# Attention's small products moved between input-projection tiles, the samples' RWKV step made a thread of the merged stage, and a written-out order table

## What is computed

```python
h = rms_norm(x, norm_mix_pre); proj = h @ w_in
q, kv_rows, win_rows, gates = nsa_project(proj[..., :NSA_PROJ], pos)      # rope on q and k, gates = sigmoid
kc, vc = compress(kv_rows[..., 0]), compress(kv_rows[..., 1])             # blocks of 32 rows, stride 16: w1, gelu, w2
o_nsa = g0 * attend(q, kc, vc) + g1 * attend_selected_blocks + g2 * attend_window
o_rwkv = rwkv_time_mix(proj[..., NSA_PROJ:])    # s = s*w + (s a) b + v k;  y = s r;  norm, gate
x = x + rms_norm(concat(o_nsa, o_rwkv) @ w_out)
x = x + rms_norm(conv_ffn(rms_norm(x)))         # conv of width 3, gelu, times value
```

## Time and profile before

| what | us |
|---|---|
| median of 3 runs | 2395.59 (2394.9 to 2395.8) |
| the profiled execution's own time | 2394.03 |
| span of its trace | 2392.2 |
| PE busy, share of the span | 2031.3, 85% |
| DVE busy | 1236.8, 52% |
| ACT busy | 715.2, 30% |
| mean granted TensorE clock | 0.919 of 2.4 GHz |

### The profile page before, as it was taken

How to read it: one execution, slowest core, us unless ns; L and a number is a source line. 1 busy time by engine, 2 the same in 40 slices (tenths; PEclk the granted TensorE clock), 3 DMA queues, 4 the chain that set the end, 5 groups by cost and what they waited for, 6 DMA issues and landing times.

```text
span 2392.2 us, 54387 instructions
## 1 busy us (share of the span) xinstructions
PE 2031.3 (85%) x22574; PEld 1861.8 (78%) x22574; DVE 1236.8 (52%) x1984; ACT 715.2 (30%) x1320; POOL 159.9 (7%) x233
## 2 busy tenths in 40 slices
PE   4997598988877899999669966989787769999995
PEld 3996587855666899999669956877566659999994
DVE  4222667778654544452332237687776454444422
ACT  3221123333333332332132221333342332222421
POOL 1000111111100001000010001110101000010000
PEclk9997699979988999999879977999899979999997
DMA  3346133223322232223122552322333212232231
GB/s 110 97 105 208 40 104 90 72 70 107 100 68 65 71 93 93 90 88 98 48 80 93 126 170 61 102 72 72 89 102 102 68 47 89 89 97 90 89 98 66
DMA packets 172769, 216.43 MB, mean 90 GB/s; under 512 B 39009, under 2 KB 138594, under 8 KB 171106
## 3 DMA queue, kind: packets, MB, share of 16 engines
q1 hardware_dynamic: 172514, 212.87, 29.7%
HBM read 204.57 MB, written 16.59 MB: 92 GB/s over the span
## 4 chain that ended last, share of the span: by engine, by line
PE 61%; DVE 18%; SPq 11%; issue 5%; ACT 3%; DMA 1%; DVEq 0%; ACTq 0%
PE ps L833 16%; PE ps L835 16%; PE ps L834 16%; SPq L713 9%; PE ps L1156 2%; PE ps L901 1%; SPq L709 1%; PE ps L874 1%; DVE x L2101 1%; PE ps L1129 1%; DVE arena L1916 1%; DVE arena L1925 1%; PE ps L1037 1%; DVE hf_lo L1654 1%; DVE arena L1690 1%
## 5 line engine op out<-in xcount | busy, mean ns | idle before, releaser
L833 PE MATMUL ps<-hm_hi,ring_hi 128*128 128x260 f32 x2432 | 694.5, 286 | 44.2 <-DVE hm_lo L1654 44.2
L835 PE MATMUL ps<-hm_hi,ring_lo 128*128 128x260 f32 x2432 | 692.3, 285 | 0.0
L834 PE MATMUL ps<-hm_lo,ring_hi 128*128 128x260 f32 x2432 | 690.3, 284 | 0.0
L1647 DVE TENSOR_TENSOR ring_lo<-ring,ring_hi 128x1024 fp32r<-128x1024 f32 x200 | 244.9, 1226 | 698.4 <-ACT ring_hi L1308 697.7
L833 PEld LDWEIGHTS ps<-hm_hi,ring_hi 128*128 128x128 f32 x2432 | 463.7, 191 | 47.9 <-issue 47.9
L834 PEld LDWEIGHTS ps<-hm_lo,ring_hi 128*128 128x128 f32 x2432 | 463.2, 190 | 0.0
L835 PEld LDWEIGHTS ps<-hm_hi,ring_lo 128*128 128x128 f32 x2432 | 463.1, 190 | 0.0
L1308 ACT ACTIVATE ring_hi<-ring 128x1024 fp32r<-128x1024 f32 x200 | 211.9, 1060 | 687.1 <-PE ps L835 674.6
L833 PE MATMUL ps<-hf_hi,ring_hi 128*128 128x260 f32 x704 | 202.2, 287 | 8.8 <-DVE hf_lo L1654 8.2
L835 PE MATMUL ps<-hf_hi,ring_lo 128*128 128x260 f32 x704 | 200.6, 285 | 0.0
L834 PE MATMUL ps<-hf_lo,ring_hi 128*128 128x260 f32 x704 | 200.5, 285 | 0.0
(11 more groups left out here) (377 smaller groups left out, 3235.3 us busy)
## 6 DMA issues: line engine op xcount, KB each, us to landing
ring<-in_w SPq DMA_DIRECT2D x202, 512.0 KB, 3.6
arena<-in_kv_cmp SPq DMA_DIRECT2D x96, 128.0 KB, 2.3
extra<-in_kv_cmp SPq DMA_DIRECT2D x80, 128.0 KB, 2.3
slot<-in_kv_cmp SPq DMA_DIRECT2D x80, 128.0 KB, 2.1
out_win_old<-in_win SPq DMA_DIRECT2D x16, 511.0 KB, 9.3
slot<-in_k_sel SPq DMA_DIRECT2D x96, 64.0 KB, 1.9
arena<-in_k_sel SPq DMA_DIRECT2D x96, 64.0 KB, 1.9
extra<-in_v_sel SPq DMA_DIRECT2D x96, 64.0 KB, 1.9
```

The costliest lines, as they stand in the source:

```text
L833: mmul(out, wh, hi[:, k, cols], start=(k == 0), stop=False)
L834: mmul(out, wh, lo[:, k, cols], start=False, stop=False)
L835: last = mmul(out, wl, hi[:, k, cols], start=False, stop=(ci == len(chunks) - 1 and k == k1 - 1))
L1647: v.tensor_tensor(ring_lo[:, n % RING, :], r, ring_hi[:, n % RING_HI, :], SUB).then_inc(S["w_lo"], 1)
```

## The change

- The 24 gate columns become a 25th full tile of the input projection, behind the attention tiles. ACT takes its tanh on the way out; PE transposes it.
- Gate transposes, rope, value transposes and the prompt's compression are given to PE, ACT and DVE between the RWKV tiles, one item behind each tile (`beside`). Their PSUM banks are 6 and 7. The compression takes the samples' paired form: 16 products instead of 64, its gelu written out with tanh and DVE operations.
- SP loads compression weights, rope table and the samples' state behind the chunk 3, and waits for the page table later. Two sample units are loaded ahead instead of three. Old window rows are copied between the sample units, after every second one.
- The samples' RWKV step becomes 23 steps in the merged order (`one_step`, `step_thread`); RWKV's first super-chunk waits for it; its two stores are issued by ACT.
- The order is written out as 750 digits, one thread number per step; the search at build time is gone.
- POOL no longer clears compression weights.

```diff
-C_IN, C_GATE = 0, NT + RP
-C_OUT = C_GATE + 1
+C_IN, N_IN = 0, NT + 1 + RP
+C_OUT = N_IN
...
-        put("mix", "DVE", 0.7, ago("rkv"))
+        put("mix", "DVE", 0.7, *([ago("rkv")] if sc else []))
+        if sc == 0:
+            key, engine, us, _ = front.pop()
+            front.append((key, engine, us, [("rs", 0, "out")]))
...
         put = into(back)
         put("scaled", "DVE", 2.72, ago(("solve", 1)), *here("exps", "keys"))
+        if sc == 0:
+            back[-1][3].append(("rs", 0, "store"))
...
+def step_thread():
+
+    out = []
+    for name, engine, us, *after in (
+            ("mix", "DVE", 2.4), ("tanh", "ACT", 0.8, "mix"), ("small", "PE", 2.6, "tanh"), ("sig", "ACT", 2.2, "small"),
+            ("root", "ACT", 0.4, "small"), ("prep", "DVE", 2.8, "sig", "root"), ("pin", "ACT", 0.4, "sig"), ("rk", "PE", 0.3, "prep"),
+            ("rks", "DVE", 0.3, "rk"), ("left", "PE", 5.4, "rks"), ("scaled", "DVE", 2.4, "left"), ("right", "PE", 4.0, "scaled"),
+            ("decay", "DVE", 4.7, "pin", "scaled"), ("add", "DVE", 4.7, "right"), ("read", "PE", 7.0, "add"), ("yc", "DVE", 0.4, "read"),
+            ("mean", "PE", 0.3, "yc"), ("msub", "DVE", 0.6, "mean"), ("var", "PE", 0.3, "msub"), ("vrec", "DVE", 0.9, "var"),
+            ("vroot", "ACT", 0.4, "vrec"), ("out", "DVE", 1.4, "vroot"), ("store", "ACT", 1.0, "out")):
+        out.append((("rs", 0, name), engine, us, [("rs", 0, a) for a in after]))
+    return out
 
 
...
-def placed(threads, favour, limit):
-
...
+ORDER = ("055067570055550060605076067655665650006666565656666556505656566565660655705060605065050716161617156516561561551166756015"
...
+def merged_order():
+
+    smp = sample_thread()
+    rows = (step_thread(), *rwkv_threads(), att_thread(), smp, load_thread(smp))
+    at, order = [0] * len(rows), []
+    for c in ORDER:
+        i = int(c)
+        key = rows[i][at[i]][0]
         at[i] += 1
...
-        w1 = at(2, BLOCK, P, reset=work0)
-        w2 = at(2, P)
-        pe_c = at(2, BLOCK)
...
+        NS = 2 * (NCP + 1) + 2
+        staged = at(2, STRIDE // 2, NS, reset=where[0] - 4 * WIN)
...
+        w1p = slots[0].rearrange("p (c k e) -> p c k e", c=2, k=STRIDE // 2)
...
-            sp.wait_ge(pages_ok, 1)
...
                     chunk(n)
-                sp.wait_ge(S["w1_zero"], 1)
-                compression_weights(l)
-                for c in range(2):
-                    for g in range(GROUPS):
-                        sp.dma_start(pe_c[g * HD:(g + 1) * HD, c, :], I["pe"][l, c]).then_inc(S["w1_ready"], 16)
-                sp.wait_ge(S["w_used"], NT + RP)
-                sp.dma_start(trig, I["trig"].rearrange("p (a t) -> p a t", a=2)).then_inc(S["trig_ok"], 16)
-
-                sp.dma_start(ss, I["wkv"][l].rearrange("p (a b c) -> p a b c", a=RJ, b=DEC)).then_inc(S["loads_s"], 16)
-                sp.wait_ge(S["w_used"], C_OUT)
-                sp.dma_start(smp[:, 0:2048], I["w1_pairs"][l]).then_inc(S["w1s_ready"], 16)
-                sp.dma_start(smp[:, 2048:2304], I["w2_pairs"][l]).then_inc(S["w1s_ready"], 16)
-                for u in range(USLOT):
+                    if n == RING:
+                        sp.dma_start(w1p, I["w1_pairs"][l].rearrange("p (c k e) -> p c k e", c=2, k=STRIDE // 2)).then_inc(S["w1_ready"], 16)
+                        sp.dma_start(w2p, I["w2_pairs"][l].rearrange("p (c e) -> p c e", c=2)).then_inc(S["w1_ready"], 16)
+                        sp.dma_start(pe_p, I["pe_pairs"][l].rearrange("p (c k h) -> p c k h", c=2, k=STRIDE // 2)).then_inc(S["w1_ready"], 16)
+                        sp.dma_start(trig, I["trig"].rearrange("p (a t) -> p a t", a=2)).then_inc(S["trig_ok"], 16)
+                        sp.dma_start(ss, I["wkv"][l].rearrange("p (a b c) -> p a b c", a=RJ, b=DEC)).then_inc(S["loads_s"], 16)
+                sp.wait_ge(S["kcp_ok"], 1)
+                sp.wait_ge(pages_ok, 1)
+                for u in range(USLOT - 1):
                     load_unit(sp, mybir.EngineType.SP, l, u)
-                sp.wait_ge(S["nsa_ready"], 1)
-                sp.dma_start(O["kv"][l].rearrange("p (a b) -> p a b", a=6), nsa[:, 4:NT, :]).then_inc(S["kv_stored"], 16)
-                for b in range(DEC):
-                    sp.dma_start(O["win_old"][l, b], I["win"][l, b]).then_inc(S["stores"], 16)
-
-                sp.wait_ge(S["rs_out"], 1)
-                sp.dma_start(O["wkv_s"][l].rearrange("p (a b c) -> p a b c", a=RJ, b=DEC), ss).then_inc(S["rs_stored"], 16)
-                sp.dma_start(O["shift"][l].rearrange("p (a b) -> p a b", a=RP), pr[:, :, SEQ:SEQ + 1 + DEC]).then_inc(S["rs_stored"], 16)
-                sp.wait_ge(S["gate_ev"], NQ + 1)
+                sp.wait_ge(S["gate_ev"], 1)
                 sp.dma_start(gate_s[:], gates[0:DEC, NQ, :].rearrange("b (h n) -> b h n", n=3)).then_inc(S["gs_ready"], 16)
                 for h in range(2):
                     for r in QROWS:
                         sp.dma_start(gate_r[r, h, :], gates[QD * h:QD * (h + 1), NQ, :].rearrange("b (h n) -> b h n", n=3)).then_inc(S["gs_ready"], 16)
-
-                for u in range(USLOT, N_UNIT):
+                sp.wait_ge(S["w_used"], C_OUT)
+                sp.dma_start(smp[:, 0:2048], I["w1_pairs"][l]).then_inc(S["w1s_ready"], 16)
+                sp.dma_start(smp[:, 2048:2304], I["w2_pairs"][l]).then_inc(S["w1s_ready"], 16)
+                sp.wait_ge(S["nsa_ready"], 1)
+                sp.dma_start(O["kv"][l].rearrange("p (a b) -> p a b", a=6), nsa[:, 4:NT, :]).then_inc(S["kv_stored"], 16)
+                for u in range(USLOT - 1, N_UNIT):
                     load_unit(sp, mybir.EngineType.SP, l, u)
+                    if USLOT <= u < USLOT + 2 * DEC and u % 2:
+                        b = (u - USLOT) // 2
+                        sp.dma_start(O["win_old"][l, b], I["win"][l, b]).then_inc(S["stores"], 16)
 
...
-                w_wait(C_GATE)
-                wg = ring[:, C_GATE % RING, 0:KB * 24].rearrange("p (k n) -> p k n", k=KB)
...
+                def beside(r):
+
+                    if r == 0:
+                        pe.wait_ge(S["gate_sg"], 1)
+                        for t in range(NQ + 1):
+                            n = P if t < NQ else DEC
+                            last = nc.tensor.transpose(ps[0:n, 6, t * 24:(t + 1) * 24], gate_rows[0:24, t * P:t * P + n], ident[0:24, 0:24])
+                        last.then_inc(S["gate_mm"], 1)
+                    elif r <= 7:
+                        if r == 1:
+                            pe.wait_ge(S["evac_a"], NT)
+                            pe.wait_ge(S["evac_v"], NT)
+                            pe.wait_ge(S["gate_ev"], 1)
+                        else:
+                            pe.wait_ge(S["rope_ok"], r - 1)
+                        for h, cols in HALVES:
+                            last = mmul(ps[:, 6 + h, 0:HALF], K("rot"), nsa[:, ROPED[r - 1], cols], start=True, stop=True)
+                        last.then_inc(S["rope_mm"], 1)
+                    elif r == 8:
+                        pe.wait_ge(S["rope_ok"], len(ROPED))
+                        for br in range(2):
+                            for t in range(NQ):
+                                last = nc.tensor.transpose(ps[:, 6 + br, t * P:(t + 1) * P], nsa[:, 7 + 2 * br, t * P:(t + 1) * P], ident)
+                        last.then_inc(S["vt_mm"], 1)
+                    elif r == 9:
+                        pe.wait_ge(S["vt_ev"], 1)
+                        pe.wait_ge(S["w1_ready"], 16 * 3)
+                        pe.wait_ge(S["staged_v"], 1)
+                        pe.wait_ge(S["staged_a"], 1)
+                        for c in range(2):
+                            for k in range(STRIDE // 2):
+                                last = mmul(ps[:, 6, c * NS:(c + 1) * NS], w1p[:, c, k, :], staged[:, c, k, :], start=(k == 0), stop=(k == STRIDE // 2 - 1))
+                        last.then_inc(S["cmpp_mm"], 1)
+                    elif r == 11:
+                        pe.wait_ge(S["cmpp_h"], 1)
+                        mmul(ps[:, 7, 0:NCP], w2p[:, 0, :], hip[:, 0, :], start=True, stop=True)
+                        mmul(ps[0:NCP, 7, P:2 * P], hip[:, 1, :], w2p[:, 1, :], start=True, stop=True).then_inc(S["cmpp_mm"], 1)
...
+                for m in range(N_IN):
+                    dense_tile([(m, 0, KB)], in_hi, in_lo, 0 if m == 0 else None)
+                    if m > NT:
+                        beside(m - NT - 1)
+                pe.wait_ge(S["evac_a"], N_IN)
+                pe.wait_ge(S["evac_v"], N_IN)
                 pe.wait_ge(S["kcp_ok"], 1)
...
+                    elif stage == "left":
+                        pe.wait_ge(S["loads_s"], 16)
+                        pe.wait_ge(S["rs_prep"], 2)
+                        for j in range(RJ):
...
+                    elif r == 9:
+                        act.wait_ge(S["cmpp_mm"], 1)
+                        o.go(A(part_p[0:HD], ps[HD:P, 6, 0:2 * NS].rearrange("p (c n) -> p c n", c=2), ACT.Copy))
...
```

(33 more changed lines are left out.)

502 lines of the change are left out of this document (228 added, 274 removed).

## The result

The changed kernel takes 2240.64 us (median of 4 runs, 2234.70 to 2247.18) against 2395.70 (2394.90 to 2400.91): a ratio of 0.9349, 95% interval 0.9318 to 0.9380. The forecast was 2254, the range 2190 to 2335. The profiled execution took 2238.46 us with a span of 2236.7, 155.5 less than the span before.

What follows compares the result with a forecast made beforehand. No engine was full in the 97 us before the merged stage; the sync engine paced that stage's second half. 2395.59 - 132.8 (two layers, 66.4 each) - 8.7 (start) = 2254 us, range 2190 to 2335.

Steps and rivals of the forecast that it cites:

- The start: Before layer 0: SP's page-table wait moves behind the compression, so norm's DVE work starts 8.7 us earlier (0 to 10), once.
- The projection: Input projection, per layer: gate tile 5.7 us, small products between tiles, and a DMA stall; its end moves from 178.50 to 201.
- The DMA stall of 2: Input projection: five loads put before weight chunk 4 delay it by 0 to 8.9 us, taken as 2.
- Up to the first selection load: Merged stage, from the projection's end: 219.6 us of old work, +22 step, -5 state pass, +4 and +3 waits, 244 total.
- The density of 0.90: Merged stage before the selection loads: TensorE's busy share stays at the old 0.90, making the step's 20 us cost 22.
- the two waits: Early merged stage: TensorE waits for pair weights, 4 us (0 to 10.2); RWKV's first DVE step for state stores, 3 (0 to 11.7).
- the missing state pass: Merged stage before the first selection load: RWKV is one state pass earlier than in the trace, -5 us (0 to 10).
- The second half: Merged stage from the second selection load: the sync engine paces it, 15 loads back to back taking 155.0 us.
- RWKV as the bound: Rival, merged stage: RWKV's 422 us cannot be packed tighter, so 28.1 us less per layer, 2331 us; chance 0.18.
- Not hidden: Rival, input projection: TensorE waits at every small product, 29 us per layer come back, 2313 us; chance 0.07.
- Busy time misleads: Rival, merged stage before the selection loads: the queue packs to the weight loads, 110.4 us less per layer, 2166 us; chance 0.10.
- The clock did not fall: Rival, merged stage: stalls lower TensorE's granted clock; at 0.75 the stage takes 525 us, total 2447 us; chance 0.05.

Runs made afterwards that it cites:

- both waits moved: Changed kernel with the nine gate loads issued before SP's wait for the compression and the shift store issued at the step's exponential: 2229.15 us, ratio 0.9306.
- 12 loads: Changed kernel with SP issuing 12 of 16 page loads per selection unit and nobody the other 4, so part of the past is unread: 2210.15 us, ratio 0.9228.
- two tables: Both waits moved, plus order tables changed by single digit moves: selection unit's load at the old duration 2232.66 us, at 10.7 us 2208.85 us.
- the run above: Changed kernel with the rounds of small products behind the projection's last tile instead of between its tiles: 2318.61 us, ratio 0.9683.
- the best table: Both waits moved, plus an order table refitted with a selection unit's load at 10.7 us: 2208.85 us, ratio 0.9218 to the kernel before.
- the run that issued the two some 5 us apart: Changed kernel with ScalarE issuing the shift store at the step's first stage instead of its last: 2241.03 us, ratio 0.9351.

## Why the prediction was right

**The start.** 8.7 forecast, 8.9 measured, but with the cause in the wrong place. The prediction said that the memsets "go at no gain of their own" and put all of it down to SP's wait. The wait alone is 2.4 us; 6.5 came from the memset, which had held up the DVE's clamp of the page table. The sum was right because the change takes both away.

**The projection.** 22.4 forecast, 17.6 measured. The gate tile is 5.6 (5.7 forecast); the products between tiles add 12.0 (14.7). By busy time, which overlaps a little with the tiles' own, rope is 7.3 (8.0), the transposes and the last two products 2.2 (3.7), the compression 3.7 (3). The DMA stall of 2 was 0: TensorE was full from 40 to 140 us. What was said to hide the rest, the slack of DVE and ScalarE per tile, did: TensorE is busy 47.25 of 47.50 us there, and with the products behind the projection 78 us return over both layers.

**Up to the first selection load.** 244 forecast, 238.8 and 240.5 measured. The density of 0.90 was met to the second digit, and the order table is part of that (below). Of the two waits, the store was taken at 3 and the DVE stood idle for 3.5 and 4.5; the pair weights were taken at 4, and with both waits moved the first load comes 5 us earlier. So the waits were worth some 5 (7 forecast), and the step less the missing state pass some 14 (233.2 - 219.6; 17 forecast); these two were not measured apart. Both waits were small for the reason given, other work lying in front, and not the 13.5 and 6.7 us that the chain of waits shows. The Trainium skill's rule (DMA: Bandwidth & Descriptors, "Issuing engines are not separate DMA queues") was right here as the prediction used it: from ScalarE the shift store took 11.0 to 13.5 us to land in the two profiles of the changed kernel, from SP 11.7, and beside it the pair weights landed later.

**The second half.** The reading that SP paces it holds by the runs with 12 loads and with two tables. The term was a little too small: 155.0 forecast, 159.3 and 162.5 measured. Layer 1 of the kernel before had 157.5 already; the forecast took layer 0 alone. The same section of the Trainium skill (DMA: Bandwidth & Descriptors, "Issuing engines are not separate DMA queues") says that the time to initiate a DMA is usually small beside the DMA itself. In this row it is not what counts: a page takes 0.51 to 0.68 us to issue and 1.9 to land, but landings overlap and issues don't.

**The table.** No term priced the search against the written-out table; the forecast read positions out of the table and took the old density. That was enough, but it hid that the table is a third of the gain: with the searched order the same change gives 2287. Had the table been no better than the search, 2254 would have been 33 us too low. That nothing in the sum stood for the table and the total still came within 14 us is luck in that term: the old density of 0.90 needed the new order. With the searched one it is 0.86 (212.59 busy of 248.60 us up to the first selection load).

**The rivals.** RWKV as the bound did not come about, since its last large operation ended at 603 us, ten before the samples; in the searched order its steps hold the samples' end back (19.7 us behind the row). "Not hidden" fell with the run above. "Busy time misleads" would have shown a density near 1.0 of weight loads; the best table reaches 0.91 and 0.90 busy products in the two windows, with weight loads at 0.80 and 0.69, so as far as these orders go the products' busy share was the nearer sign of the limit. That no order packs closer is not shown. The Trainium skill (Trainium Kernel Development and Optimization, "Best Practices") names weight-load busy share, beside the share of peak arithmetic, and not matmul busy share as the measure; in these two windows the other share fits better. The prediction's "full DVE" for 280 to 500 is not in its rows: the DVE was busy 165.87 of 220 us. The clock did not fall: 0.91 ahead of the loads, 0.97 in the row.

## What to carry to other kernels

Small dependent products cost least between the tiles of a dense stage: there they took 12 us; behind it, with TensorE idle between them and a granted clock of 0.57, they took 41. A row of transfers that one queue issues back to back gets shorter by fewer transfers and otherwise only starts earlier, so a planner should carry the real issue time per transfer: the table refitted with 1.1 us more per unit came out 9 us per layer shorter, the one refitted at the old price no shorter. A long row in the chain of waits is a latency, and the idle time in front of the waiting instruction says better what it costs: two such rows of 20 us together stood in front of 4.4 us of idle time in layer 0, and with both waits moved the first selection load came 5 us earlier.

## What the hardware showed that was not expected

A DVE operation on one partition and 128 integers took 6.91 us while POOL cleared 128 x 8192 elements, started 0.15 us earlier, in 6.99; without the memset it took 0.21. The Trainium skill (SBUF — State Buffer, "Who interferes with whom") says that a DVE `tensor_scalar` can run in a mode that uses a port pair shared with POOL, and that whoever issues first has the pair for the whole instruction while the other blocks. The two rows agree with that; which mode the operation ran in, no row shows. A store of 63 KB in short pieces (nine columns of each of 14 tiles in every partition) took 11.0 to 13.5 us to land in the changed kernel, where a load of 1 MB took 6.0. In the run that issued the two some 5 us apart, the load took 8.2 and 8.7.
